# Full-width heads in two mixers of a four-layer kernel: padded values, 128-row scores with the forget term among them, and both masks of a group ahead

## The reference, cut to what matters

```python
def causal_softmax_attention(q, k, v, scale, decay=None):
    ...                               # per block of 128 queries
        logits = einsum('bhqd,bhkd->bhqk', qb, k) * scale
        if decay is not None:
            logits = logits + cq[..., :, None] - decay[..., None, :]
        p = softmax(where(k_idx <= q_idx, logits, NEG_INF))
        return einsum('bhqk,bhkd->bhqd', p, v)

def stick_breaking_attention(q, k, v):
    ...
        z = einsum('bhqd,bhkd->bhqk', qb, k) * scale      # then, strictly causal:
        a = where(mask, exp(log_sigmoid(z) + suffix), 0.0)
        return einsum('bhqk,bhkd->bhqd', a, v)

def odd_mixer(h, w_in, f_bias, q_norm, k_norm, w_o):      # the last mixer
    q, k, v, f_logit = split_last(h @ w_in, [1024, 1024, 1024, 16])
    ...                                                   # q and k normalised per head
    decay = cumsum(log_sigmoid(f_logit + f_bias), axis=1)
    return merge_heads(causal_softmax_attention(q, k, v, 64 ** -0.5, decay)) @ w_o
```

## Time and profile before

| | us |
|---|---|
| median of three runs | 929.55 (929.50 to 929.56) |
| the profiled execution | 929.66 |
| its span, first to last instruction | 927.6 |
| PE busy | 913.1 (98%) |
| PE weight loads | 775.7 (84%) |
| DVE busy | 590.1 (64%) |
| ACT busy | 496.4 (54%) |
| POOL busy | 42.7 (5%) |

### The profile page before, as it was taken

The page is one execution under the profiler, slowest core; times in us unless marked ns, Lnnn a source line. Parts: engine busy times, 40 slices in busy tenths (PEclk is TensorE's granted clock), DMA queues, the critical chain, the costliest instruction groups (busy, mean ns, idle before and its releaser), DMA issues.

```text
span 927.6 us, 14273 instructions
## 1 busy us (share of the span) xinstructions
PE 913.1 (98%) x5404; PEld 775.7 (84%) x5404; DVE 590.1 (64%) x1018; ACT 496.4 (54%) x869; POOL 42.7 (5%) x77
## 2 busy tenths in 40 slices
PE   8999999999999999999999999999999999999998
PEld 5999998899899998777888888888777788888886
DVE  5887778674756777478555554556888665555443
ACT  5468543554665656566444444545676654444441
POOL 2003300000000013000000000010000000000000
PEclk9999999999999999999999999999999999999999
DMA  9545431556335465124556655664443455555560
GB/s 334 186 137 165 122 114 57 194 167 240 122 109 164 159 185 169 45 92 137 183 183 188 189 190 185 195 185 160 158 133 97 135 182 181 181 182 185 182 198 23
DMA packets 106296, 148.25 MB, mean 160 GB/s; under 512 B 12565, under 2 KB 59345, under 8 KB 106113
## 3 DMA queue, kind: packets, MB, share of 16 engines
q1 hardware_dynamic: 104334, 145.61, 48.9%
q0 software_dynamic: 704, 1.77, 0.5%
q10 hardware_dynamic: 1202, 0.13, 0.1%
HBM read 146.03 MB, written 1.45 MB: 159 GB/s over the span
## 4 chain that ended last, share of the span: by engine, by line
PE 87%; DVE 6%; ACT 5%; issue 1%; DMA 1%; DVEq 0%; ACTq 0%
PE ps L1888 25%; PE ps L1890 24%; PE ps L1889 24%; PE ps L1988 4%; DVE wlo L1183 2%; ACT whi L674 2%; ACT f_s L1099 1%; PE ps L2144 1%; PE ps L2293 1%; PE ps L2370 1%; DMA x<-in_x 1%; DVE G L1355 1%; PE ps L2135 0%; DVE f_s L1808 0%; PE ps L2072 0%
## 5 line engine op out<-in xcount | busy, mean ns | idle before, releaser
L1183 DVE TENSOR_TENSOR wlo<-raw,whi 128x1024 fp32r<-128x1024 f32 (+1 forms) x271 | 319.4, 1219 | 213.3 <-ACT whi L674 213.0
L674 ACT ACTIVATE whi<-raw 128x1024 fp32r<-128x1024 f32 (+1 forms) x271 | 270.1, 1045 | 270.0 <-PE ps L1890 269.9
L1888 PE MATMUL ps<-whi,xh 128*128 128x512 f32 (+1 forms) x544 | 217.6, 400 | 0.9 <-DVE wlo L1183 0.6
L1890 PE MATMUL ps<-whi,xl 128*128 128x512 f32 (+1 forms) x544 | 211.8, 389 | 0.0
L1889 PE MATMUL ps<-wlo,xh 128*128 128x512 f32 (+1 forms) x544 | 211.5, 389 | 0.0
L1888 PEld LDWEIGHTS ps<-whi,xh 128*128 128x128 f32 x544 | 102.2, 188 | 22.6 <-issue 2.6
L1890 PEld LDWEIGHTS ps<-whi,xl 128*128 128x128 f32 x544 | 102.1, 188 | 21.6
L1889 PEld LDWEIGHTS ps<-wlo,xh 128*128 128x128 f32 x544 | 102.4, 188 | 18.6
L1888 PE MATMUL ps<-xh,whi 128*128 128x256 f32 x384 | 111.8, 291 | 0.7 <-DVE xl L1249 0.3
L1890 PE MATMUL ps<-xh,wlo 128*128 128x256 f32 x384 | 108.6, 283 | 0.0
L1889 PE MATMUL ps<-xl,whi 128*128 128x256 f32 x384 | 108.6, 283 | 0.0
(11 more groups left out here) (396 smaller groups left out, 1157.8 us busy)
## 6 DMA issues: line engine op xcount, KB each, us to landing
raw<-in_l_w_gate SPq DMA_DIRECT2D x44, 512.0 KB, 3.8
raw<-in_l_w_up SPq DMA_DIRECT2D x44, 512.0 KB, 4.7
raw<-in_l_w_down SPq DMA_DIRECT2D x44, 512.0 KB, 4.6
raw<-in_l_w_in SPq DMA_DIRECT2D x36, 512.0 KB, 4.2
raw<-in_a_w_in SPq DMA_DIRECT2D x32, 512.0 KB, 4.6
raw<-in_w_kv SPq DMA_DIRECT2D x16, 512.0 KB, 4.7
raw<-in_b_w_in SPq DMA_DIRECT2D x16, 512.0 KB, 4.5
raw<-in_l_w_o SPq DMA_DIRECT2D x16, 512.0 KB, 4.3
```

What stands on the lines that cost most here:

```text
L674: nc.scalar.activation(whi[:, g % HIGH, a], raw[:, g % RAW, a], ACT.Copy).then_inc(hi_done, 1)
L1183: nc.vector.tensor_tensor(wlo[:, g % LOW, a], raw[:, g % RAW, a], whi[:, g % HIGH, a].bitcast(F32), ALU.subtract).then_inc(lo_done, 1)
L1888: mm(o_, a_h, b_h, start=start, stop=False, skip_group_check=True)
L1890: return mm(o_, a_l, b_h, start=False, stop=stop, skip_group_check=True)
```

## The change

Four things change; the tables of slots stay as they are.

1. **Values.** `f_v`, `m_v` and `sb_v` (now in `xn`) hold for each head 128 columns, its 64 and 64 zeros, set once by POOL (`between_heads`). `pair_values` multiplies both heads of a pair with 128-column weights into the same 128 partitions, the second adding to the first.
2. **Scores of the last mixer.** `f_qkT` becomes `f_q` and `f_k` with 128 rows a head: 64 rows of the head, one row for the forget term (ones in `f_q`, the running sum in `f_k`), the other rows zero. `f_sel`, `f_pick` and `f_cT` go. The running sum has 16 rows, DVE reads it with one operation into `f_c`, POOL's queue writes that to DRAM, and after that write has landed reads it back into one row of `f_k` for even heads and one for odd: two transfers for heads 0 to 7, two more for heads 8 to 15 when the scores of heads 0 to 7 are done. PE waits for the rows ahead of heads 0 and 8.
3. **ACT.** Each copy of transposed q and k becomes two, of 64 partitions each. Copies that overwrite `f_q` and `f_k` wait for scores, those that fill the second half of `f_v` wait for values.
4. **Masks.** In a group of stick-breaking heads both mask products come first, then the products of head one, then those of head two.

```diff
+        f_q = sb("f_q", [P, 2, 4, T], F32, lay)
+        f_k = sb("f_k", [P, 2, 4, T], F32, lay)
+        f_c = sb("f_c", [16, T], F32, lay)
...
+        own = lambda t: t.rearrange("p t (a c d) -> p t a c d", c=4, d=64)[:, :, :, 0:4:3, :]
+        between_heads = lambda t: t.rearrange("p t (a f) -> p t a f", f=T)[:, :, :, 64:192]
+        padded = lambda t, kt, e: t[:, kt, P * (e % 8):P * (e % 8) + P]
...
+            pool.wait_ge(*past("nc", "ss", 2 * NT))
+            for t in (m_v, sb_v):
+                nc.gpsimd.memset(between_heads(t), 0.0).then_inc(S("masks"), 1)
...
-            nc.gpsimd.tensor_copy(f_sel[:], f_pick[:].unsqueeze(2).to_broadcast([112, 16, P])).then_inc(S("f_sel"), 1)
+            nc.gpsimd.memset(between_heads(f_v), 0.0).then_inc(S("f_pads"), 1)
...
+            pool.wait_ge(S("f_c"), 1)
+            pool.dma_start(fox_rows, f_c[:]).then_inc(S("f_rows"), 16)
+            pool.wait_ge(S("f_rows"), 16)
+            for n in range(2):
+                if n:
+                    pool.wait_ge(*past("f", "sc", 4))
+                for o, r in enumerate((64, 0)):
+                    pool.dma_start(f_k[r:r + 1, o], bass.AP(fox_rows.tensor, (8 * n + o) * T, [[T, 1], [2 * T, 4], [1, T]]))\
+                        .then_inc(S("f_rows"), 16)
...
-                    nc.scalar.activation(f_qkT[:, f:f + 2, :].rearrange("p a t -> p (a t)"), ps[:, 6 + (r if c < 2 else 0), :],
-                                         ACT.Copy, scale=gain_fox(f // KT)).then_inc(step("f", "pTs"), 1)
+                    if c >= 3:
+                        act.wait_ge(*past("f", "sc", 2 * r + 2))
+                    for o, rows_ in enumerate(HALVES):
+                        last = nc.scalar.activation((f_k if f >= KT else f_q)[rows_, o, 2 * r:2 * r + 2, :].rearrange("p a t -> p (a t)"),
+                                                    ps[rows_, 6 + (r if c < 2 else 0), :], ACT.Copy, scale=gain_fox(f // KT)[rows_])
+                    last.then_inc(step("f", "pTs"), 1)
...
-                    for to, src in keys:
-                        link(nc.vector.tensor_scalar(f_cT[:, to], ps[0:112, 5, src], -8.0, None, ALU.mult))
...
+                    nc.vector.tensor_scalar(f_c[:], ps[0:16, 5, 0:T], -8.0, None, ALU.mult).then_inc(S("f_c"), 1)
...
+            def pair_values(o_, v, h, p):
+
+                for n in range(2):
+                    mm(o_, padded(v, 0, h + n), p[n][:, 0:T], start=n == 0, stop=False, skip_group_check=True)
+                    last = mm(o_[:, P:T], padded(v, 1, h + n), p[n][:, T:3 * P], start=False, stop=n == 1, skip_group_check=True)
+                return last
...
                     for n in range(2):
+                        mm(z_[:, 0:3 * P]..., eye_r, strict_r..., start=True, stop=False, skip_group_check=True)
+                    for n in range(2):
                         k_, q_ = half(sbT[:, 4 + i], n), half(sbT[:, i], n)
                         z_ = ps[:, SB_BANK[i] + n, :]
-                        mm(z_[:, 0:3 * P]..., eye_r, strict_r..., start=True, stop=False, skip_group_check=True)
...
-                    for e in (h, h + 1):
-                        r, v = slice(64 * (e % 2), 64 * (e % 2) + 64), f_v[:, :, 64 * e:64 * e + 64]
-                        mm(ps[r, 7, 0:T], v[:, 0], f_pT[:, e % 4, 0:T], start=True, stop=False, skip_group_check=True)
...
+                    last = pair_values(ps[:, 7, 0:T], f_v, h, [f_pT[:, e % 4] for e in (h, h + 1)])
...
-                        pe.wait_ge(S("f_cT"), 4)
-                        pe.wait_ge(S("f_sel"), 1)
+                        pe.wait_ge(S("f_pads"), 7)
+                    if h in (0, 8):
+                        pe.wait_ge(S("f_rows"), 4 * h + 48)
...
                     for e in (h, h + 1):
-                        mm(ps[:, 4 + e % 2, 0:3 * P], f_sel[low(e, 48), e, :], f_cT[low(e, 48), :], start=True, stop=False,
-                           skip_group_check=True)
...
+                        q_, k_ = f_q[:, e % 2, e // 2 % 4], f_k[:, e % 2, e // 2 % 4]
+                        for tt in range(NT):
+                            last = mm(ps[:, 4 + e % 2, SPAN[tt]], q_[:, P * tt:P * tt + P], k_[:, 0:P * (tt + 1)], start=True, stop=True)
```

More of the change, by code:

```diff
@@ L163, in block_kernel @@
         m_qk = sb("m_qk", [P, NT, 16, MLA_QK], F32, lay)
-        m_kv = sb("m_kv", [P, NT, HEADS, 64], F32, lay)
+        m_v = sb("m_v", [P, NT, D], F32, lay)
         m_qkT = sb("m_qkT", [P, 16, T], F32, lay)
@@ L456, in block_kernel @@
         scratch = nc.dram_tensor("bias_rows", (HEADS, 3 * P), F32, kind="Internal").ap()
+        fox_rows = nc.dram_tensor("fox_rows", (16, T), F32, kind="Internal").ap()
         NB = P // SUB
@@ L648, in _ @@
             pool.wait_ge(acc_read["D"], read_by("D", J_DN[0] + 1))
[L649 to L654, removed]
-            nc.gpsimd.tensor_copy(f_sel[:], f_pick[:].unsqueeze(2).to_broadcast([112, 16, P])).then_inc(S("f_sel"), 1)
+            nc.gpsimd.memset(between_heads(f_v), 0.0).then_inc(S("f_pads"), 1)
+            pool.wait_ge(S("f_pads"), 1)
+            pads = 1
+            for t in (f_q, f_k):
+                for o, r in enumerate((HALVES[1], HALVES[0])):
+                    nc.gpsimd.memset(t[r, o], 0.0).then_inc(S("f_pads"), 1)
+                    pads += 1
+            pool.wait_ge(S("f_pads"), pads)
+            nc.gpsimd.memset(f_q[64:65, 0], 1.0).then_inc(S("f_pads"), 1)
+            nc.gpsimd.memset(f_q[0:1, 1], 1.0).then_inc(S("f_pads"), 1)
+            pool.wait_ge(S("f_c"), 1)
[7 more added lines that the diff above has]
+                        .then_inc(S("f_rows"), 16)
         @block.scalar
@@ L895, in evacuate @@
                 for tt in range(NT):
-                    last = nc.scalar.activation(to[:, tt], ps[:, bank(j0 + c) + tt, :], ACT.Copy, scale=r[:, tt:tt + 1])
+                    o_ = ps[:, bank(j0 + c) + tt, :]
+                    last = nc.scalar.activation(to[:, tt], o_ if name == "nb" else in_pairs(o_), ACT.Copy, scale=r[:, tt:tt + 1])
                 last.then_inc(acc_read["A"], 1)
@@ L1006, in mixer @@
                         nc.scalar.activation(m_sq_k[:, tt], kv[:, :, 0:64], ACT.Square).then_inc(S("kv_read"), 1)
-                        nc.scalar.activation(m_kv[:, tt], kv[:, :, 64:128], ACT.Copy).then_inc(S("kv_read"), 1)
+                        nc.scalar.activation(own(m_v)[:, tt], kv[:, :, 64:128].rearrange("p (a c) d -> p a c d", c=2),
+                                             ACT.Copy).then_inc(S("kv_read"), 1)
                     hi_until(U_LQ + 1)
@@ L1046, in _ @@
                 if s == 24:
-                    evacuate("nc", U_SV, J_SV, 0, sb_v[:])
+                    evacuate("nc", U_SV, J_SV, 0, own(sb_v))
                 if s % 4 == 0:
@@ L1103, in fox @@
                     if i is None:
-                        n = c // 3
-                        evacuate("nd", U_D, J_D, c, f_v[:, :, 512 * n:512 * n + 512])
+                        if c == 5:
+                            act.wait_ge(*past("f", "pv", 4))
+                        evacuate("nd", U_D, J_D, c, own(f_v))
                         continue
@@ L2361, in mixer @@
                         pe.wait_ge(S("kv_read"), 4 + NT)
-                        pe.wait_ge(S("masks"), 2)
+                        pe.wait_ge(S("masks"), 4)
                     if i == 3:
@@ L2388, in mixer @@
                         pe.wait_ge(S("sb_out"), g - 1)
[L2389 to L2392, removed]
-                        last = mm(ps[r, 2 + g % 2, P:T], v_[:, 1], p_[:, T:3 * P], start=False, stop=True,
-                                  skip_group_check=True)
+                    last = pair_values(ps[:, 2 + g % 2, 0:T], sb_v, 2 * g, [sb_a[g][:, n, :] for n in range(2)])
                     last.then_inc(S("sb_pv"), 1)
@@ L2399, in mixer @@
                         pe.wait_ge(*past("m", "out_sb", h // 2))
-                    for e in (h, h + 1):
-                        r = slice(64 * (e % 2), 64 * (e % 2) + 64)
-                        mm(ps[r, 7, 0:T], m_kv[:, 0, e], m_pT[:, e % 2, 0:T], start=True, stop=False, skip_group_check=True)
-                        last = mm(ps[r, 7, P:T], m_kv[:, 1, e], m_pT[:, e % 2, T:3 * P], start=False, stop=True,
-                                  skip_group_check=True)
+                    last = pair_values(ps[:, 7, 0:T], m_v, h, [m_pT[:, n] for n in range(2)])
                     last.then_inc(step("m", "pv"), 1)
```

43 lines of the change are left out of this document (10 added, 33 removed).

## The result

The changed kernel took 935.61 us (median of four runs, 934.61 to 936.86) against 929.55 (929.50 to 929.56): a ratio of 1.0066, 95% interval 1.0054 to 1.0078. It is slower, by 6.06 us; the forecast was 934.0 with a range of 930.9 to 937.2. Five more runs of the same kernel, made later, gave 936.24 (936.15 to 938.26). The times of the nine lie in groups: two runs at a mean granted clock of 1.000 took 934.61 and 934.84, the seven others, at 0.998 or 0.996, took 936.15 to 938.26. The profiled execution is the one of 934.61 us (span 932.8), so its rows show the change without the fall of the clock.

A forecast was written before the change was run, and what follows sets the result against it. TensorE (PE) was taken as the bound, working 69.42 of 70 us in the last mixer's window. Values +2.7 and +2.0, scores +0.6, masks -4.2, forget rows +3.2 sum to +4.3: 929.66 becomes 934.0 us, range 930.9 to 937.2.

The forecast's parts named there:

- Values: Padded value products of head pairs: +0.34 us a pair, +2.7 in the last mixer (no slack), +2.0 in the MLA mixer.
- The double block: Two sb_v pairs in one MLA-mixer slot: at least +1.0 us for both, about 0.3 taken up by PE's zl wait.
- the last one: Last value block of the MLA mixer: its 0.34 us goes into PE's wait for zl of an earlier pair.
- The wait for m_pT: In the MLA mixer, a 0.76 us PE wait behind one value block takes up that block's 0.34 us.
- Scores: Last mixer, eight pairs, 128-row passes without selecting product: 1.76 against 1.69 us, +0.07 a pair, +0.6 in all.
- Masks: Four stick-breaking groups, both masks first: heads run side by side in row halves, -1.04 us a group, -4.2 in all.
- Forget rows: Round trip through DRAM before the last mixer's first scores: PE stands 3.2 us, bounds 0 and 5.
- What was put at nothing: POOL's memsets, DVE's changed operations, ACT's new waits and the 16-column cumulative products: no cost expected.
- +3.3 for the rest of the last mixer: Last mixer's values, +2.7 us, and scores, +0.6, without the forget rows.
- The 16-column sums: Running-sum products on PE, now 16 columns wide: as many as before, so no cost.
- The likeliest case: Whole kernel, the forecast itself: 934.0 us, own range 932.3 to 936.0, chance 0.58.
- Rival D: PE's clock falls during the stand at the last mixer's first scores: about +1.6 us, 935.6, chance 0.12.

## Why the prediction was right, and where not

- **Direction and range: right.** Slower, 935.61 in 930.9 to 937.2.
- **Values: the price right, the MLA mixer's sum in part by luck.** 0.34 us a pair forecast, 0.35 measured in the last mixer. In the MLA mixer +2.0 and +2.06 agree by errors that cancel. The double block, put at +0.7, cost nothing, since the wait for zl went altogether. Against that, two single blocks cost 0.59 and 0.54 instead of 0.34, which was not followed up, and the last one, put at nothing, cost 0.33: 0.07 at once and 0.26 behind the next products, where PE now waits for the last part of zl. The wait for m_pT gave back 0.42, as argued. The claim that the last mixer has no slack is too strong: about 0.7 us of waits were there to be filled.
- **Scores: right.** 0.07 a pair forecast, 0.08 measured in most. A form that another mixer already used carried its price over to here.
- **Masks: the mechanism right, one group mis-sized.** Row halves do run side by side when issued head by head. The term that failed is "-1.04 a group, -4.2 in all": the step looked whether POOL's multiplication would move up with PE (it did: it ends at 370.50, PE asks at 370.78), and overlooked the suffix sums of the third group, whose soft-plus on DVE starts 2.0 us earlier (372.64 in place of 374.65) where PE comes 3.2 earlier. The fourth group gave 0.33.
- **Forget rows: right by two errors that cancel.** The write took 4.92 us (653.24 to 658.16) where 4.0 was taken from the earlier trace rows; the read landed 1.7 us after its issue where the earlier trace rows gave 3.0. f_c was there at 652.95, as forecast once the 1.15 us are taken off by which PE ran ahead there. The stand of 2.84 us with its slow entry makes 3.1.
- **What was put at nothing: right but for two, of which the second is the next point.** POOL's zeros and ones were set by 623.75, 29 us before f_c. But ACT's copies in two halves, counted only as a delay of f_c, made PE wait once and cost it 0.35 us. That +3.20 still came so near to +3.3 for the rest of the last mixer is luck in part: this term, and the waits that the longer blocks filled, go opposite ways.
- **The 16-column sums: missed.** Taken as costing nothing, they cost PE 0.3 us, which the stand hid.
- **The likeliest case was not the one that happened most.** The terms measured above, without the clock, are those of the times 934.6 and 934.8, seen in two of nine executions. Rival D (935.6, chance 0.12) is what the median shows: in the other seven the clock falls, for about 1.5 us. D had the fall during the stand; in the one trace that shows it for this kernel it comes 1.4 us after the stand's end. Its chance was too low; the argument against it was only that no row showed a stand of 3 us. Taking the stand away removed the fall and lengthening it to 7.6 us brought it in every run, so the stand as its cause is shown. What decides it from execution to execution is open: the one with the fall stood 2.75 us, those without 2.84 and 2.97. That D's price came out right is luck in part. It was worked out from six products at the start that took 4.25 us in the earlier trace rows; the same six in the changed kernel's trace would have given 2.9 in place of 1.6, and the view lists a granted clock of 1.00 there in both:

```profile
1.21 5.49 PE L2030 MATMUL ps<-rbc 128*128 128x512 f32 x6 [1.21 <-DVE rbc L1276]
```

## What to carry to other kernels

Two heads in the halves of the array (rows or columns) run side by side, so padding them to full width cost 0.35 us a pair here, although two changes of shape went; count what runs together before you remove a switch of shape. Put what breaks such a pair apart (a mask, a selecting product) ahead of both. And when a change makes a full engine stand, price not only the stand but the clock behind it, look whether the engine that prepares its operands has more to do (the divided copies), and look for a path without the round trip: a copy from SBUF to SBUF took 2.5 us of stand away here.

## What the runs showed of the hardware

Behind a stand of about 3 us (2.75 to 2.97 in three traces, of two kernels) the execution's mean granted clock was 0.996 to 0.998 in 15 of 18 executions and 1.000 in three. Behind one of 7.6 us it was 0.996 in all four; behind 0.4 to 0.9 us it was 0.999 or above in all 24 executions of three kernels. The two traces with a lower mean show the fall itself, to 0.50. The Trainium skill, "TensorE: Matmul & The Clock Gate", Part 1, has TensorE go back to the half clock when it is left idle. These runs agree in all four executions with the longest stand and in most of those with about 3 us. Behind 2.75 us the clock fell only after PE had worked for 1.4 us again, and came back 3.4 us later, in the middle of uninterrupted products. And a product with 16 output columns costs more at its edges than one with 112: 0.3 us for a block of three. ACT took 0.68 us for a copy of 512 columns on 64 partitions and 0.69 for one on 128, so dividing it by partitions doubled its time.
